# Moving operands of TensorE placed 64 bytes short of the weights' residue modulo 256

## Chip, cores and metric

One core of one Trainium2 chip. The metric is device time in microseconds (us) of one execution. All work is in fp32: matrix products are made of three products of a tighter 4-byte format (fp32r), as told below.

## What is computed

One layer of a macaron block on x of 512 tokens by 1024 channels, then a last RMS norm:

```python
x = x + 0.5 * swiglu(rms_norm(x, ffn1_norm), w_gate1, w_up1, w_down1)      # 1024 -> 2816 -> 1024
h = rms_norm(x, mix_norm)
z, xbc, dt_raw, u = split(h @ w_in)                                       # 1024 -> 3600
y_ssd = ssd_group(z, xbc, dt_raw, ...)     # conv of 4 taps, SiLU, chunked scan of 16 heads, gate, group norm
y_pool = pool_group(u, ...)                # trailing means of 2/4/8/16 frames, 256x256 maps
x = x + concat(y_ssd, y_pool) @ w_out                                     # 2048 -> 1024
x = x + 0.5 * swiglu(rms_norm(x, ffn2_norm), w_gate2, w_up2, w_down2)
out = rms_norm(x, final_norm)
```

## The kernel before

Everything is kept with channels on the 128 partitions and the 512 tokens along a row, so that one tile of 128 channels is 2048 bytes of each partition. `xT` holds the eight tiles of x.

**Units.** The weights come in 199 units. A unit is 8 blocks of 128 by 128 (5 or 6 for the down projections), fetched by SyncE's queue into one of RING = 4 slots of `raw` (`fetch`). ScalarE rounds it into `whi` (line 498, `convert`), VectorE subtracts into `wlo` (line 743), and TensorE multiplies. Activations are split likewise: `xghi`/`xglo` for the input of a stage, `acthi`/`actlo` for the hidden layer of the two feed-forward parts, `mixhi`/`mixlo` for the output of the SSD group, `sp0`..`sp2` for the pooled channels.

**Products.** `products` is the inner loop of nearly all of it. For each block k of a unit it makes three matmuls of 512 columns into one PSUM bank: weights `whi` with moving `hi` (line 1150), `whi` with `lo` (line 1151), `wlo` with `hi` (line 1152). Each has its own weight load of 128 columns, recorded as PEld, which the chip starts while the matmul ahead of it streams. A unit of 8 blocks is 24 such matmuls. The opening (`part`, lines 1216, 1219, 1222) makes the first 96 of them in another order, the dt unit 16 with narrow weights, the pool maps 48 (lines 1406 to 1408), and the very last tile 132 with 256 columns (lines 1471 to 1473), in two halves of the tokens with the tile's transposes between.

**Order.** Opening and gate/up of the first feed-forward (moving `xghi`, `xglo`, to some 253 us), its down projection (`acthi`, `actlo`, to 377), the mixer (`xghi`, `xglo` again, with small transposes of line 1274, decay rows, states of line 1284 and scans between the units; then `mixhi`, `mixlo` from 622 to 666), gate/up of the second feed-forward (`xghi`, to 907) and its down projection (`acthi`, to the end). The order of work on each engine is written out by hand and held by semaphores; it has no planner.

**Addresses.** The tensors of `sb(...)` are stacked one after another in each partition. The allocator puts the first, `raw`, at byte 1152. `raw`, `whi`, `wlo`, `xT`, `xghi`, `xglo` are 16,384 bytes each:

| tensor | start | start modulo 256 | role in TensorE |
|---|---|---|---|
| `whi`, `wlo` | 17536, 33920 | 128 | weights; a block is 512 bytes |
| `xghi`, `xglo` | 66688, 83072 | 128 | moving; a tile is 2048 bytes |
| `sumsq`, `ones`, `ident`, `causal` | 105600 to 108672 | 128 | weights or moving |
| `base` | 110016 | 192 | start of everything below |
| `acthi`, `actlo` | base, base + 44 KB | 192 | moving |
| `mixhi`, `mixlo`, `sp0`..`sp2`, `xsT`, `bT`, `ebuf`, `cbuf`, `acs_split`, `xst` | base + whole multiples of 256 | 192 | moving, or weights of transposes |

`base` is the end of the stack rounded up to a multiple of 64. All blocks and tiles are multiples of 256 bytes long, so every operand of these tensors has the residue of its tensor. The last tensor on `base` ends at 226,496; the allocator's limit is 229,368.

Of the kernel before, what the change touches and what calls it, by code (L numbers as in the profile page):

```python
# [23 lines left out]
P = 128  # L24
# [23 lines left out]

RING = 4
UB = 8  # L50
DOWN = (6, 6, 5, 5)
DOWN0 = (0, 6, 12, 17)

# [46 lines left out]
def block(tile):  # L100
    return slice(tile * P, (tile + 1) * P) if isinstance(tile, int) else bass.ds(tile * P, P)
# [6 lines left out]
def build(nc, t, out):  # L108
    with ExitStack() as ctx:
        def sb(name, shape, dt=F32):  # L110
            return ctx.enter_context(nc.sbuf_tensor(name, shape, dt))
# [4 lines left out]

        raw = sb("w_raw", [P, RING, UB, P])
        whi = sb("w_hi_part", [P, RING, UB, P], F32R)
        wlo = sb("w_lo_part", [P, RING, UB, P], F32R)
        xT = sb("xT", [P, DK * S])  # L120
        xghi = sb("xghi", [P, DK * S], F32R)
        xglo = sb("xglo", [P, DK * S], F32R)
        rstd = sb("rstd", [P, S])
# [13 lines left out]
        tok_rms = sb("tok_rms", [P, 2, NC])  # L137


        base = (nc.sbuf_base + 63) // 64 * 64  # L140

        def at(name, offset, shape, dt=F32):
            return nc.alloc_sbuf_tensor_at(name, shape, dt, offset=base + offset)
# [112 lines left out]
        def slot(m):  # L256
            return m % RING
# [27 lines left out]
        def _(sp):  # L285
            def fetch(m, i, src, blocks=UB, width=P):

                sp.wait_ge(w_hi, i * RING + (m - RING + 1))
                sp.wait_ge(w_lo, i * RING + (m - RING + 1))
                dst = raw[:, slot(m), 0:blocks, :]  # L290
                if width != P:
                    dst = raw[:, slot(m), :, :].rearrange("p (g c) n -> p g (c n)", c=width // P)
                sp.dma_start(dst, src).then_inc(landed[slot(m)], 16)

            def ffn_fetch(f, m0):
# [10 lines left out]
                with sp.Fori(0, DK) as i:  # L306
                    for j in range(4):
                        fetch(m0 + N_GU + j, i, wd[f][:, DOWN0[j]:DOWN0[j] + DOWN[j], block(i)], DOWN[j])

# [12 lines left out]
            def half_weight(m, h):  # L322
                ks = slice(h * (UB // 2), (h + 1) * (UB // 2))
                sp.dma_start(raw[:, m, ks, :], (wg, wu)[m % 2][0][:, ks, block(m // 2)]).then_inc(
                    (half_landed, landed)[h][m], 16)
# [163 lines left out]
        def _(act):  # L489
# [44 lines left out]
            def first_hi_half(m, h):  # L534

                act.wait_ge((half_landed, landed)[h][m], 16)
                ks = slice(h * (UB // 2), (h + 1) * (UB // 2))
                act.activation(whi[:, m, ks], raw[:, m, ks], ACT.Copy).then_inc((first_hi, w_hi)[h], 1)
# [597 lines left out]
        def _(pe):  # L1136
            def products(bank, m, i, blocks, hi, lo, k0, first=True, last=True, ready=None,
                         order=None, midway=None):

                pe.wait_ge(w_hi, i * RING + (m + 1))  # L1140
                pe.wait_ge(w_lo, i * RING + (m + 1))
                s = slot(m)
                for n, k in enumerate(order or range(blocks)):
                    if midway and n == blocks // 2:
                        midway()
                    if ready:
                        pe.wait_ge(ready[0], ready[1] + n + 1)
                    h, l = hi[:, cols(k0 + k)], lo[:, cols(k0 + k)]
                    w, wl = whi[:, s, k, :], wlo[:, s, k, :]
                    pe.matmul(bank, w, h, start=first and n == 0, stop=False)  # L1150
                    pe.matmul(bank, w, l, start=False, stop=False)  # L1151
                    mm = pe.matmul(bank, wl, h, start=False, stop=last and n == blocks - 1)  # L1152
                mm.then_inc(unit_done, 1)
# [17 lines left out]
            def down(f, m0, i, behind=None, tiles=2):  # L1171
                for e in range(tiles):
                    d = i * 2 + e
                    for j in range(4):
                        if j == 0:
# [3 lines left out]
                            else:  # L1179
                                pe.wait_ge(x_ready, d + (DK * (2 * f + 1) - 1))  # L1180
                        pe.wait_ge(act_lo, FT * f + DOWN0[j] + DOWN[j])
                        products(PB[4 + e][:, :], m0 + N_GU + 4 * e + j, i * 2, DOWN[j], acthi, actlo, DOWN0[j],
                                 first=j == 0, last=j == 3)
# [277 lines left out]
            for h in range(2):  # L1461
                for j in range(4):
                    m = M_FFN2 + N_GU + 4 * (DK - 1) + j
                    pe.wait_ge(w_hi, m + 1)
                    pe.wait_ge(w_lo, m + 1)
                    for k in range(DOWN[j]):
                        t0 = (DOWN0[j] + k) * S + h * HALF
                        hi, lo = acthi[:, t0:t0 + HALF], actlo[:, t0:t0 + HALF]
                        bank = PB[LAST_BANK[h]][:, 0:HALF]
                        first, last = j == 0 and k == 0, j == 3 and k == DOWN[3] - 1  # L1470
                        pe.matmul(bank, whi[:, slot(m), k, :], hi, start=first, stop=False)  # L1471
# [30 lines left out]
```

## Time and profile before

| | |
|---|---|
| median of 2 runs | 1041.89 us (1041.59 to 1042.2) |
| the profiled execution: its own time | 1042.32 us |
| its span from first to last instruction | 1040.6 us |
| granted TensorE clock, mean | 0.997 of 2.4 GHz |
| busy: PE, PEld, DVE, ACT, POOL | 1031.2, 847.3, 559.6, 380.4, 179.1 us |
| data moved by DMA | 99.09 MB, 95 GB/s over the span |

PE is TensorE's matmuls, PEld its weight loads, DVE VectorE, ACT ScalarE, POOL GpSimd. A matmul's booked duration overlaps the next one's, and its end is modelled; the distance between two starts says how fast a stream runs. PEclk is the clock that the chip granted to TensorE, as a share of 2.4 GHz.

### The profile page before, as it was taken

To read this page: it belongs to the slowest core of one execution; us is meant where nothing else is said; L and a number is where in the kernel's file an instruction comes from. 1 tells how busy PE (TensorE), PEld (TensorE's weight loads), DVE (VectorE), ACT (ScalarE), POOL (GpSimd) and SP (SyncE) were. 2 spreads that over 40 slices of the span, in tenths; PEclk is the share of its full clock that TensorE was granted. 3 is DMA by queue.
4 is the path that set the end of the run, shared out by engine and by line. 5 is a ranking of instruction groups with operands and counts; after the bars stand their busy time and mean duration, and the time that the engine had idled before them with its cause. 6 is when DMAs were issued, how large, how long until landed. Compare 5 with 4: busy or idle time off the path is not lost.

```text
span 1040.6 us, 13577 instructions
## 1 busy us (share of the span) xinstructions
PE 1031.2 (99%) x4798; PEld 847.3 (81%) x4798; DVE 559.6 (54%) x686; ACT 380.4 (37%) x489; POOL 179.1 (17%) x166
## 2 busy tenths in 40 slices
PE   9999999999999999999999999999999999999997
PEld 7888888888888878878787888888888888888887
DVE  5544444444344468786799795554444444433432
ACT  6433223322333337652234753432333223332332
POOL 1110110101001032221063451110101101101100
PEclk9999999999999999999999999999999999999998
DMA  6533323322333343222222233333333332233222
GB/s 184 150 113 101 101 86 95 101 83 68 99 98 96 101 124 100 82 81 70 73 81 81 62 101 101 101 101 90 92 101 101 96 87 89 79 109 95 86 68 81
DMA packets 188873, 99.09 MB, mean 95 GB/s; under 512 B 3780, under 2 KB 188200, under 8 KB 188840
## 3 DMA queue, kind: packets, MB, share of 16 engines
q1 hardware_dynamic: 188168, 97.60, 32.3%
q10 hardware_dynamic: 672, 1.05, 0.3%
q8 instruction: 21, 0.34, 0.1%
q14 instruction: 12, 0.10, 0.0%
HBM read 96.54 MB, written 2.10 MB: 95 GB/s over the span
## 4 chain that ended last, share of the span: by engine, by line
PE 96%; DVE 3%; issue 1%; ACT 1%; POOL 0%; ACTq 0%; POOLq 0%
PE bank L1150 29%; PE bank L1152 29%; PE bank L1151 29%; PE bank L1222 1%; PE bank L1216 1%; PE bank L1219 1%; PE bank L1471 1%; PE bank L1284 0%; PE bank L1306 0%; PE bank L1472 0%; PE bank L1473 0%; PE bank L1274 0%; DVE w_lo_part L743 0%; DVE ebuf L903 0%; PE bank L1190 0%
## 5 line engine op out<-in xcount | busy, mean ns | idle before, releaser
L1150 PE MATMUL bank<-xghi,w_hi_part 128*128 128x512 f32 x960 | 377.4, 393 | 0.0
L1152 PE MATMUL bank<-xghi,w_lo_part 128*128 128x512 f32 x960 | 373.8, 389 | 0.0
L1151 PE MATMUL bank<-xglo,w_hi_part 128*128 128x512 f32 x960 | 373.6, 389 | 0.0
L743 DVE TENSOR_TENSOR w_lo_part<-w_raw,w_hi_part 128x1024 fp32r<-128x1024 f32 x194 | 253.9, 1309 | 192.8 <-ACT w_hi_part L498 187.5
L498 ACT ACTIVATE w_hi_part<-w_raw 128x1024 fp32r<-128x1024 f32 x194 | 203.8, 1051 | 196.2 <-PE bank L1152 194.7
L1150 PEld LDWEIGHTS bank<-xghi,w_hi_part 128*128 128x128 f32 x960 | 180.2, 188 | 39.9 <-issue 2.8
L1151 PEld LDWEIGHTS bank<-xglo,w_hi_part 128*128 128x128 f32 x960 | 180.3, 188 | 38.4 <-issue 1.2
L1152 PEld LDWEIGHTS bank<-xghi,w_lo_part 128*128 128x128 f32 x960 | 180.2, 188 | 37.5
L1150 PE MATMUL bank<-acthi,w_hi_part 128*128 128x512 f32 x330 | 130.5, 396 | 0.0
L410 POOL TENSOR_TENSOR gate_buf<-gate_buf,rstd 128x512 f32<-128x512 f32 x44 | 57.1, 1298 | 424.5 <-ACT gate_buf L521 424.5
L1152 PE MATMUL bank<-acthi,w_lo_part 128*128 128x512 f32 x330 | 129.4, 392 | 0.0
L1151 PE MATMUL bank<-actlo,w_hi_part 128*128 128x512 f32 x330 | 128.1, 388 | 0.0
L524 ACT ACTIVATE acthi<-act 128x512 f32 (+1 forms) x44 | 27.8, 632 | 170.9 <-DVE act L766 170.9
L521 ACT ACTIVATE gate_buf<-gate_buf 128x512 f32<-128x512 f32 x44 | 27.8, 632 | 150.5 <-DVE gate_buf L763 150.5
L397 POOL TENSOR_TENSOR sumsq<-sumsq,sq 128x512 f32<-128x512 f32 x23 | 32.8, 1427 | 257.8 <-ACT sq L509 257.8
L1152 PEld LDWEIGHTS bank<-acthi,w_lo_part 128*128 128x128 f32 x330 | 61.9, 188 | 14.5
L1151 PEld LDWEIGHTS bank<-actlo,w_hi_part 128*128 128x128 f32 x330 | 62.0, 188 | 13.6
L1150 PEld LDWEIGHTS bank<-acthi,w_hi_part 128*128 128x128 f32 x330 | 62.0, 188 | 12.2
L766 DVE TENSOR_TENSOR act<-bank,gate_buf 128x512 f32<-128x512 f32 x44 | 30.4, 690 | 71.1 <-PE bank L1152 68.9
L763 DVE TENSOR_TENSOR gate_buf<-bank,rstd 128x512 f32<-128x512 f32 x44 | 30.4, 691 | 62.7 <-PE bank L1152 62.6
L768 DVE TENSOR_TENSOR actlo<-act,acthi 128x512 f32 (+1 forms) x44 | 30.5, 693 | 39.7 <-ACT acthi L524 39.7
L748 DVE SCALAR_TENSOR_TENSOR xglo<-xT,par,xghi (+1 forms) x24 | 25.6, 1078 | 25.6 <-ACT xghi L502 25.5
(223 smaller groups left out, 805.0 us busy)
## 6 DMA issues: line engine op xcount, KB each, us to landing
w_raw<-in_ffn_w_gate SPq DMA_DIRECT2D x42, 512.0 KB, 3.8
w_raw<-in_ffn_w_up SPq DMA_DIRECT2D x42, 512.0 KB, 3.8
w_raw<-in_w_in SPq DMA_DIRECT2D x29, 512.0 KB, 3.8
w_raw<-in_ffn_w_down SPq DMA_DIRECT2D x32, 384.0 KB, 3.2
w_raw<-in_ffn_w_down SPq DMA_DIRECT2D x32, 320.0 KB, 3.0
w_raw<-in_w_out SPq DMA_DIRECT2D x16, 512.0 KB, 3.6
out<-xtok SPq DMA_DIRECT2D x4, 512.0 KB, 3.4
xload<-in_x SPq DMA_DIRECT2D x3, 512.0 KB, 7.0
```

The lines of the kernel that those rows point to most:

```text
L397: pool.tensor_tensor(sumsq[:, :], sumsq[:, :], sq[:, e, :], ALU.add).then_inc(sum_own, 1)
L410: pool.tensor_tensor(gsilu[:, e, :], gsilu[:, e, :], rstd[:, :], ALU.mult).then_inc(g_r, 1)
L498: act.activation(whi[:, slot(m)], raw[:, slot(m)], ACT.Copy).then_inc(w_hi, 1)
L521: act.activation(gsilu[:, e, :], gscaled[:, e, :], ACT.Silu).then_inc(g_silu, 1)
L524: act.activation(acthi[:, cols(i * 2 + e)], act32[:, e, :], ACT.Copy).then_inc(act_hi, 1)
L743: dve.tensor_tensor(wlo[:, slot(m)], raw[:, slot(m)], whi[:, slot(m)].bitcast(F32), ALU.subtract).then_inc(w_lo, 1)
L763: dve.tensor_tensor(gscaled[:, e, :], PB[j][:, :], rstd[:, :], ALU.mult).then_inc(g_scaled, 1)
L766: dve.tensor_tensor(act32[:, e, :], PB[j][:, :], gsilu[:, e, :], ALU.mult).then_inc(act_ready, 1)
L768: dve.tensor_tensor(actlo[:, cols(i * 2 + e)], act32[:, e, :], acthi[:, cols(i * 2 + e)].bitcast(F32), ALU.subtract).then_inc(act_lo, 1)
L1150: pe.matmul(bank, w, h, start=first and n == 0, stop=False)
L1151: pe.matmul(bank, w, l, start=False, stop=False)
L1152: mm = pe.matmul(bank, wl, h, start=False, stop=last and n == blocks - 1)
```

## The change

Three edits, all to addresses. A tensor of padding, 48 elements or 192 bytes a partition, is put on the stack after `xT` so that `xghi` begins at residue 128 + 192 = 320, that is 64, modulo 256. `xglo` and all that is stacked behind it follow: `ones`, `ident`, `causal`, `sumsq` too come to 64. `base` is rounded up to the next address of residue 64 and not to the next multiple of 64; it goes from 110016 to 110400, so that all tensors on it move by 384 bytes. `raw`, `whi`, `wlo` and `xT` stay where they are. No instruction is added, removed or moved.

```diff
@@ -48,6 +48,8 @@
 
 RING = 4
 UB = 8
+LANES = 256
+WEIGHT_LANE = 128
 DOWN = (6, 6, 5, 5)
 DOWN0 = (0, 6, 12, 17)
 
@@ -118,6 +120,13 @@
         whi = sb("w_hi_part", [P, RING, UB, P], F32R)
         wlo = sb("w_lo_part", [P, RING, UB, P], F32R)
         xT = sb("xT", [P, DK * S])
+        def start_at(residue):
+
+            lane = (residue - nc.sbuf_base) % LANES
+            if lane:
+                sb(f"lane{nc.sbuf_base}", [P, lane // 4])
+
+        start_at(WEIGHT_LANE + 192)
         xghi = sb("xghi", [P, DK * S], F32R)
         xglo = sb("xglo", [P, DK * S], F32R)
         rstd = sb("rstd", [P, S])
@@ -137,7 +146,7 @@
         tok_rms = sb("tok_rms", [P, 2, NC])
 
 
-        base = (nc.sbuf_base + 63) // 64 * 64
+        base = nc.sbuf_base + (WEIGHT_LANE + 192 - nc.sbuf_base) % LANES
 
         def at(name, offset, shape, dt=F32):
             return nc.alloc_sbuf_tensor_at(name, shape, dt, offset=base + offset)
```

## Rows read from the trace of the kernel before

**Rows 1.** The page: busy us by engine, and the chain that ended last.

```profile
PE 1031.2 (99%) x4798; PEld 847.3 (81%) x4798; DVE 559.6 (54%) x686; ACT 380.4 (37%) x489; POOL 179.1 (17%) x166
...
PE 96%; DVE 3%; issue 1%; ACT 1%; POOL 0%; ACTq 0%; POOLq 0%
```

**Rows 2.** Waits of TensorE: us in total, times, longest.

```profile
PE bank L1190 <- POOL ones L368: 1.1, 1, 1.1
PE bank L1222 <- DVE w_lo_part L781: 0.6, 1, 0.6
...
PE bank L1216 <- ACT xghi L502: 0.3, 1, 0.3
```

**Rows 3.** Three stretches of TensorE: length, busy (count), PEclk, DMA share, GB/s.

```profile
98.00:250.00 152.00, 152.00 (x672) 1.00 0.31 91
256.00:370.00 114.00, 114.00 (x499) 1.00 0.35 102
740.00:900.00 160.00, 160.00 (x707) 1.00 0.31 91
```

**Rows 4.** Line 1150 in 98:135 and 255:372: durations min/median/max, first and last start.

```profile
L1150 PE MATMUL bank<-xghi,w_hi_part x55: 389/389/389, 98.2 to 134.9; 128*128 128x512 f32 x55
...
L1150 PE MATMUL bank<-acthi,w_hi_part x171: 394/394/394, 254.6 to 371.4; 128*128 128x512 f32 x171
```

**Rows 5.** Timeline of TensorE from 402 to 407: start us, booked us.

```profile
402.60 0.60 PE L1274 MATMUL bank<-ident,bT 128*128 128x128 f32 x4
...
403.27 0.39 PE L1151 MATMUL bank<-xglo,w_hi_part 128*128 128x512 f32 x1
...
404.65 0.39 PE L1151 MATMUL bank<-xglo,w_hi_part 128*128 128x512 f32 x1
404.88 0.39 PE L1152 MATMUL bank<-xghi,w_lo_part 128*128 128x512 f32 x1
...
406.92 0.39 PE L1152 MATMUL bank<-xghi,w_lo_part 128*128 128x512 f32 x1
```

**Rows 6.** The page's groups and its DMA issues (KB, us to landing).

```profile
L743 DVE TENSOR_TENSOR w_lo_part<-w_raw,w_hi_part 128x1024 fp32r<-128x1024 f32 x194 | 253.9, 1309 | 192.8 <-ACT w_hi_part L498 187.5
...
L763 DVE TENSOR_TENSOR gate_buf<-bank,rstd 128x512 f32<-128x512 f32 x44 | 30.4, 691 | 62.7 <-PE bank L1152 62.6
...
w_raw<-in_ffn_w_gate SPq DMA_DIRECT2D x42, 512.0 KB, 3.8
```

**Rows 7.** TensorE's groups by form: count, busy us, mean ns, idle before.

```profile
L1150 PE MATMUL bank<-xghi,w_hi_part 128*128 128x512 f32 x960 | 377.4, 393 | 0.0
...
L1150 PE MATMUL bank<-acthi,w_hi_part 128*128 128x512 f32 x330 | 130.5, 396 | 0.0
...
L1150 PE MATMUL bank<-mixhi,w_hi_part 128*128 128x512 f32 x64 | 25.2, 394 | 0.0
...
L1471 PE MATMUL bank<-acthi,w_hi_part 128*128 128x256 f32 x44 | 12.4, 282 | 0.0
...
L1216 PE MATMUL bank<-xghi,w_hi_part 128*128 128x512 f32 x32 | 10.4, 421 | 0.3 <-ACT xghi L502 0.3
...
L1284 PE MATMUL bank<-xst,btok 128*128 128x512 f32 x12 | 5.8, 592 | 0.0
```

**Rows 8.** Timeline of TensorE at 449.67: four matmuls of line 1284 merged.

```profile
449.67 1.88 PE L1284 MATMUL bank<-xst,btok 128*128 128x512 f32 x4
```

**Rows 9.** Timeline of TensorE in the last tile's two halves, then PEld's share.

```profile
1018.43 0.28 PE L1471 MATMUL bank<-acthi,w_hi_part 128*128 128x256 f32 x1
...
1021.83 0.28 PE L1471 MATMUL bank<-acthi,w_hi_part 128*128 128x256 f32 x1
...
1028.10 0.28 PE L1471 MATMUL bank<-acthi,w_hi_part 128*128 128x256 f32 x1
...
1030.93 0.28 PE L1471 MATMUL bank<-acthi,w_hi_part 128*128 128x256 f32 x1
...
1019.00:1025.00 6.00, 6.00 (x55) 6.00 (x54) 0.42 (x1) 0.67 (x2) 0.26 (x1) 1.00 0.00 0
```

## Prediction

> **What bounds the kernel now.** I read the page from the top. TensorE is busy for 1031.2 of 1040.6 us, VectorE for 54% and ScalarE for 37%; the chain of work that ended last is 96% TensorE [rows 1]. The waits of TensorE for other engines are next: there are six, 3.2 us in all, the longest 1.1 us at the very start and the shortest 0.3 [rows 2]. So time goes only if the matmuls follow each other faster. Busy time cannot say that, because a matmul of 512 columns is booked at 389 ns while the next starts after 227; I therefore count starts.
>
> At the clock granted in the long stretches (1.00 of 2.4 GHz, [rows 3]) 512 columns at one a cycle are 512/2.4 = 213.3 ns. With `xghi`/`xglo` as moving operand, line 1150 starts 55 times from 98.2 to 134.9 us, and three matmuls lie between two of its starts: 36.7/(54x3) = 226.5 ns. The finer timeline gives 404.88 to 406.92 us over 9 matmuls: 226.7. With `acthi`/`actlo`, line 1150 starts 171 times from 254.6 to 371.4: 116.8/(170x3) = 229.0 ns [rows 4, 5]. Counting whole stretches gives the same order: 160 us hold 707 matmuls (226 ns) with `xghi`, 114 us hold 499 (228 ns) with `acthi`, at the same clock [rows 3]. Only the address differs in a way I can name. The weight blocks begin at residue 128 modulo 256; `xghi` also does (relation 0), `acthi` at 192 (relation +64). So the relation can plausibly cost 2.3 ns of 227, though two stages differ in more than this.
>
> **The change part by part.** *Instructions and waits.* None is added or removed: two address shifts, +192 bytes from `xghi` on and +384 for everything on `base`. The last tensor then ends at 226,880, below the allocator's limit of 229,368. Cost 0. *Other engines' operands* move by multiples of 64 bytes. Were ScalarE, VectorE or GpSimd a few per cent slower by it, it would lie under TensorE: a unit of 24 products lasts 24 x 227 = 5.4 us, and VectorE works in it for one 1309 ns subtraction and, in the gate/up stages, on average one and a half passes of 690 ns: 2.3 us [rows 6]. Even at 213 ns a matmul the unit is 5.1 us. DMAs of a unit land in 3.8 us, four units ahead. I take 0, range 0 to 1 us (the waits of rows 2 a third longer).
>
> *Relation of moving operand to weights*, the real term. Counts [rows 6, 7]: relation 0 now: 3x960 (`xghi`), 3x32 in the opening, 16 of the dt unit: 2992 matmuls of 512 columns. Relation +64 now: 3x330 (`acthi`), 3x64 (`mixhi`), 48 pool products: 1230, and 132 of 256 columns. All come to -64, which no 512-column stream of this trace has. The 128-column transposes go the other way, from -64 (`ident` against `xsT`) to 0; some 110 of them at 109 ns start to start [rows 5] are 12 us, and 5% of that either way is 0.6 us: I take 0. Bounds from rows:
> - Lower: nothing lost at all. The one 512-column form that reads slower, plain f32 at line 1284, takes 1.88 us for four, of which the last is booked at 592: (1880-592)/3 = 429 ns, or 214.7 per 512 cycles [rows 7, 8]. Then 2992 x 12.0 + 1230 x 14.2 = 35.9 + 17.5 = 53 us less.
> - Upper: the slow state that the trace does show. The 256-column products of the last tile run at (1021.83-1018.43)/30 = 113.3 ns in the first half and (1030.93-1028.10)/24 = 117.9 ns in the second, with one residue and one code [rows 9]. 117.9 is 10.5% over its 106.7; 512 columns at that rate are 235.8. After an interruption 512-column products also run slower and then settle: six of them in 403.27 to 404.65 us, 230 ns each, before the 226.7 [rows 5]. Then 2992 x 9.1 + 1230 x 6.8 = 27.2 + 8.4 = 36 us more.
> - Between: 226.7 ns is 17/16 of 213.3, and 113.3 is 17/16 of 106.7. Two widths and two relations (0, +64) reach the same 17/16; that speaks for a rate of the 4-byte stream itself, one cycle per 16 columns, with collisions with weight reads on top (0 at relation 0 once settled, 2.3 ns at +64). It is no proof: with 256 columns PEld is booked for the whole of 1019 to 1025 [rows 9], so 113.3 may be the weight loads' own pace.
>
> I take the floor of 17/16 for all: 1230 x (229.0-226.7 = 2.3) = 2.8 us, and 84 of the 132 half-width ones from 117.9 to 113.3, 0.4 us: 3.2 us less. The settling after interruptions I leave as it is: 6 x 3.3 = 20 ns a place, so that sixty places would be 1.2 us. The profiled execution has 1042.3 us, 1.7 above its span and 0.4 above the median 1041.9: 1042.3 - 3.2 = 1039.1, on the median 1038.7. I say 1039.
>
> Here a rule speaks against the change having any effect. The two stages above differ by 2.3 ns a matmul. The Trainium skill (SBUF — State Buffer, "Who interferes with whom") says that TensorE has two independent read ports, one for the moving operand and one for weights, and never waits on anyone; by it the sum is 0 and the time stays 1042. The rows agree that busy neighbours do not matter, and leave open why 227 and 229 differ.
>
> **The rivals.**
> *B: the 17/16 is itself a collision, and -64 takes it away.* A weight block is 512 bytes; if its reads and the moving reads go through the same lanes, 13.4 ns may be what each load costs, and moving operands that trail by a lane may miss it. For: the trace's relation seems to matter already; plain f32, which takes twice the time per column, loses only 1.4 ns per 213. Against: 17/16 at both widths and both relations seen; settled stages show the loss in every matmul, whichever of the two weight tensors is loaded. All of it gone is 1042 - 53 = 989; half is 1015; I price it at 1000.
> Beside it: the Trainium skill (TensorE: Matmul & The Clock Gate, "Back-to-back issue gap") gives N/2.4 + 2.5 = 215.8 ns for an isolated bf16 gap; by it 2992 x 10.9 + 1230 x 13.2 = 49 us go, for 993. No settled 512-column row here reaches it.
> *C: -64 behaves as +64.* All relation-0 streams go from 226.7 to 229.0: 2992 x 2.3 = 6.9 us, nothing gained elsewhere: 1049. For: it is the nearest relation in size. Against: whether the moving read leads or trails the weight read need not be symmetrical.
> *D: slower.* With the moving read a lane behind, it runs into the weight read from the start of every load and never settles: the state that now lasts some six matmuls after an interruption, or all of the second half in rows 9, becomes permanent. Place: the inner products, lines 1150 to 1152. Price up to 36 us: 1078; it decides for "slower" from 232.3 ns a matmul (2992 x 5.6 + 1230 x 3.3 = 21 us). For: such a state is in the trace and lasted over 4 us in the last tile. Against: both relations seen leave it in 512-column streams.
> *E: the address has no effect* (the two stages differ by something else, such as the distance between high and low halves): 1042.
>
> **How the numbers follow.** A, the floor everywhere, 1039: 0.34. B, 989 to 1015: 0.26. C, 1049: 0.18. D, 1064 to 1078: 0.12. E, 1042: 0.10. The two per cent that a measurement can tell from no change is 21 us. B gives faster 0.26; A, C and E give same 0.62; D gives slower 0.12. The range: from 1039 down into B, leaving out only its full removal (about 0.1), and up past C to the foot of D (about 0.08 left out): 995 to 1060. The likeliest case alone spans 1036 to 1042 (with the transients gone, or 226.7 reached only in part).
>
> **What would show it.** Right: line 1150 to 1152 booked at 389 ns with `acthi` and `mixhi` too (now 394 settled); starts 226.7 apart in all stages; the first down projection (528 products, 121 us) 1.2 us shorter; gate/up stages unchanged. B: all of them booked below 389 and over 720 starts in a 160 us stretch of gate/up. C: 392 to 397 in the `xghi` groups, in a repeating triple like 232, 226, 229. D: 397 or more, and no settling after the transposes. The prediction is wrong if the `xghi` stages change by more than 1 ns a matmul, since the floor is what I carry over to a residue that no row shows; a change of VectorE's or ScalarE's mean durations with new waits of TensorE would refute the step that costs these at nothing.

## The result, and the profile after

| | before | changed |
|---|---|---|
| median | 1041.89 us | 1064.55 us |
| ratio, 95% interval | | 1.0216 (1.0199 to 1.0232) |
| span of the profiled execution | 1040.6 | 1063.1 |
| granted clock | 0.997 | 0.998 |

The kernel became 22.7 us slower. The prediction said 1039 and no more than 1060: it was wrong in size and in sign. The page of the changed kernel, busy time and the chain that ended last (lines of the kernel are now nine further down: 1150 to 1152 are 1159 to 1161):

```profile
PE 1054.1 (99%) x4798; PEld 847.5 (80%) x4798; DVE 559.5 (53%) x686; ACT 380.5 (36%) x489; POOL 179.0 (17%) x166
...
PE 98%; DVE 1%; ACT 0%; issue 0%; POOL 0%; ACTq 0%; POOLq 0%
```

Against [rows 1] one number moved: PE, from 1031.2 to 1054.1, 22.9 us, as much as the whole kernel lost. VectorE, ScalarE, GpSimd and the weight loads are as busy as before to 0.2 us, and the instructions are as many. TensorE's waits (us in total, times, longest):

```profile
PE bank L1199 <- POOL ones L377: 1.1, 1, 1.1
PE bank L1231 <- DVE w_lo_part L790: 0.6, 1, 0.6
...
PE bank L1225 <- ACT xghi L511: 0.3, 1, 0.3
```

All stand in [rows 2] too, with the same lengths; there are five now, 2.8 us in all, where there were six, 3.2 us. So nobody keeps TensorE waiting longer than before; its own stream runs slower. The three stretches of [rows 3], and line 1159 in 98 to 135 us (durations min/median/max, first and last start):

```profile
98.00:250.00 152.00, 152.00 (x654) 1.00 0.31 91
256.00:370.00 114.00, 114.00 (x490) 1.00 0.32 96
740.00:900.00 160.00, 160.00 (x688) 1.00 0.31 92
```

```profile
L1159 PE MATMUL bank<-xghi,w_hi_part x54: 393/396/398, 97.6 to 134.7; 128*128 128x512 f32 x54
```

At the same granted clock 160 us now hold 688 matmuls and held 707; the `acthi` stretch holds 490 and held 499. Line 1159 starts every (134.7-97.6)/(53x3) = 233.3 ns, where [rows 4] gave 226.5, and its booked durations spread over 393 to 398 where they all were 389. The timeline around the same transposes as in [rows 5]:

```profile
411.33 0.39 PE L1161 MATMUL bank<-xghi,w_lo_part 128*128 128x512 f32 x1
...
412.27 0.60 PE L1283 MATMUL bank<-ident,bT 128*128 128x128 f32 x4
412.62 0.48 PE L1159 MATMUL bank<-xghi,w_hi_part 128*128 128x512 f32 x1
412.94 0.40 PE L1160 MATMUL bank<-xglo,w_hi_part 128*128 128x512 f32 x1
...
415.74 0.40 PE L1160 MATMUL bank<-xglo,w_hi_part 128*128 128x512 f32 x1
```

From 412.94 to 415.74 are 12 matmuls, 233.3 ns each, from the first on; before, six at 230 led over to 226.7. The four transposes are booked for 0.60 us together as before, although their relation went from -64 to 0. Summed over the whole trace from each start to the next of any matmul, the three lines with `xghi`/`xglo` took 658.1 us before and 675.7 now (+17.6), with `acthi`/`actlo` 227.2 and 231.5 (+4.3), with `mixhi`/`mixlo` 44.0 and 44.8 (+0.8), and the half-width products 16.1 and 15.9 (-0.3 unrounded). Together that is 22.4 of the 22.5 us by which the spans differ.

### The profile page after: what moved, and what is told of

Read it like the earlier page. It is cut to its first block, busy times and chain, and to the rows that moved or that the text cites. A ratio compares the mean times of both kernels' runs of the same rounds, so it can differ in the third digit from the quotient of the medians.

```text
span 1063.1 us, 13577 instructions
## 1 busy us (share of the span) xinstructions
PE 1054.1 (99%) x4798; PEld 847.5 (80%) x4798; DVE 559.5 (53%) x686; ACT 380.5 (36%) x489; POOL 179.0 (17%) x166
## 4 chain that ended last, share of the span: by engine, by line
PE 98%; DVE 1%; ACT 0%; issue 0%; POOL 0%; ACTq 0%; POOLq 0%
PE bank L1159 30%; PE bank L1160 30%; PE bank L1161 30%; PE bank L1315 1%; PE bank L1231 1%; PE bank L1225 1%; PE bank L1228 1%; PE bank L1320 0%; PE bank L1293 0%; PE bank L1480 0%; PE bank L1481 0%; PE bank L1482 0%; PE bank L1283 0%; PE bank L1199 0%; PE bank L1415 0%; PE bank L1215 0%
## 5 line engine op out<-in xcount | busy, mean ns | idle before, releaser
L1159 PE MATMUL bank<-xghi,w_hi_part 128*128 128x512 f32 x960 | 383.0, 399 | 0.0
L1160 PE MATMUL bank<-xglo,w_hi_part 128*128 128x512 f32 x960 | 379.6, 395 | 0.0
L1161 PE MATMUL bank<-xghi,w_lo_part 128*128 128x512 f32 x960 | 379.6, 395 | 0.0
L1160 PE MATMUL bank<-actlo,w_hi_part 128*128 128x512 f32 x330 | 130.4, 395 | 0.0
```

## Experiments

The theory now: what counts is the distance, modulo 256, from the residue of the weights to that of the moving operand (the relation). Rivals: the absolute residue 64 is bad; or the two stages of the kernel before differed for another reason.

**Both kinds at relation 0** (all_0). Edits are shown against the changed kernel, here and below.

```diff
-        start_at(WEIGHT_LANE + 192)
+        start_at(WEIGHT_LANE + 0)
...
-        base = nc.sbuf_base + (WEIGHT_LANE + 192 - nc.sbuf_base) % LANES
+        base = nc.sbuf_base + (WEIGHT_LANE + 0 - nc.sbuf_base) % LANES
```

> All moving operands at relation 0 to the weights (residue 128, base too). Relation theory (the distance of moving operand and weights modulo 256 sets the rate; relation 0 runs at 226.7 ns a matmul, +64 at 229, -64 at 233.3): acthi and mixhi streams fall from 229.0 to 226.7, xghi stays; 1230 x 2.3 = 3 us less than before: 1039. Rival, what made acthi slower than xghi in the kernel before is something else (distance of high and low halves, stage): 1042, acthi still at 229.

Measured: 1040.43 us against 1042.33 for the kernel before, ratio 0.9983 (0.9973 to 0.9992). Line 1159 in the down projection, and the last tile (start, booked):

```profile
L1159 PE MATMUL bank<-acthi,w_hi_part x172: 389/389/389, 255.2 to 371.5; 128*128 128x512 f32 x172
```

```profile
1018.11 0.28 PE L1480 MATMUL bank<-acthi,w_hi_part 128*128 128x256 f32 x1
...
1021.71 0.28 PE L1480 MATMUL bank<-acthi,w_hi_part 128*128 128x256 f32 x1
```

The `acthi` stream went to (371.5-255.2)/(171x3) = 226.7 ns. Of the 3 us, 2 arrived: the 512-column products took 2.4 us less, but the half-width ones, at (1021.71-1018.11)/30 = 120.0 ns, are slower than either state of [rows 9] and took 0.6 us more. Of the relations tried in the whole kernel, 0 is the best place for 512 columns and a bad one for 256.

**The same relation -64 at other absolute residues** (weights_up): 64 bytes of padding ahead of `raw`, so that the weights begin at 192 and the moving operands at 128.

```diff
+        sb("lane_w", [P, 16])
         raw = sb("w_raw", [P, RING, UB, P])
...
-WEIGHT_LANE = 128
+WEIGHT_LANE = 192
```

> Weights move to residue 192 and all moving operands to residue 128, so the relation is again -64 but no absolute residue is that of the change. Relation theory: as the changed kernel, 1064 to 1065, 233 ns a matmul. Rival, the absolute residue of the moving operand decides (128 is good, 64 bad): 226.7 ns and 1039 to 1042.

Measured: 1064.69 us, ratio 1.0216 (1.0199 to 1.0233), the same as the changed kernel. The inner products of the gate/up stage (`whi` with `xghi`, now line 1160) have the spread and the starts of the changed kernel's:

```profile
L1160 PE MATMUL bank<-xghi,w_hi_part x54: 393/396/398, 97.6 to 134.7; 128*128 128x512 f32 x54
```

The residue 128 of the moving operand, good before, is as bad as 64 once the weights are at 192. So the residue of the moving operand alone does not decide. Case E of the prediction, that addresses do nothing, was refuted by the change itself.

**Relations +128 and +64 for all** (all_p128, all_p64), by the numbers in the two lines of the first diff.

> All moving operands at relation +128 (residue 0). No row shows it. Relation theory with collisions that depend on who leads: between the values of +64 and -64, 229 to 233 ns, 1048 to 1065. Rival, the distance alone counts and 128 is farthest: either free of collisions, at or under 226.7 ns and 1039 or less, or the worst, over 1065. Absolute residue theory gives no number.

> All at relation +64, the price of the prediction's case C. Sweep: xghi streams 2992 x 2.3 = 7 us more, less up to 1 us for settling: 1048 to 1049, with a triple like 232, 226, 229 in the gate/up stages. Rival, the value 229 belongs to the down projections alone: 1042, 227 in the gate/up stages.

Measured: 1062.65 us, ratio 1.0203 (1.0186 to 1.022), at +128, inside the 1048 to 1065 of the relation theory and outside both of the rival's; 1048.11 us against 1042.00, ratio 1.006 (1.0043 to 1.0077), at +64, as the theory said. The same stretch, 740 to 900 us, of these two (+128, then +64):

```profile
740.00:900.00 160.00, 160.00 (x688) 1.00 0.32 93
```

```profile
740.00:900.00 160.00, 160.00 (x701) 1.00 0.31 91
```

The gate/up stages at +64 show the triple that [rows 4]'s down projection averages, near 226, 229 and 232 ns. At +128 the streams have no single value: over 24 matmuls without an interruption they take between 232.1 and 233.3 ns, where the kernel with all at 0 has 226.7 and the changed one 233.3 nearly everywhere.

**One part at a time** (xg_only, base_only).

In xg_only `xghi` and `xglo` stay at -64 and `base` goes back to +64; in base_only it is `xghi` that goes back, to 0.

```diff
-        base = nc.sbuf_base + (WEIGHT_LANE + 192 - nc.sbuf_base) % LANES
+        base = nc.sbuf_base + (WEIGHT_LANE + 64 - nc.sbuf_base) % LANES
```

```diff
-        start_at(WEIGHT_LANE + 192)
+        start_at(WEIGHT_LANE + 0)
```

> Only xghi, xglo and what is stacked behind them move to relation -64; base keeps +64. If the relation costs what the sweep shows (226.7 at 0, 233.3 at -64), the xghi streams lose 2992 x 6.6 = 20 us, less about 1 us because the settling phases of the kernel before are already as slow: 1060 to 1062, and acthi stays at 229. Rival, the loss of the changed kernel sits in the down projections and the mixer's other products: 1042 to 1047.

> Only base moves, from relation +64 to -64; xghi and xglo keep 0. Sweep: 1230 x (233.3 - 229.0 = 4.3) = 5 us more, less 0.3 us for the half-width products of the last tile: 1046 to 1047. The two one-part kernels should add up to the changed kernel's 22 us. Rival, the parts interact (transposes between weights on base and ident): they add up to less or more by over 3 us.

Measured: 1059.26 and 1047.28 us against 1042.00, ratios 1.0165 (1.0148 to 1.0182) and 1.0053 (1.0036 to 1.007). 17.3 + 5.3 = 22.6 us, the changed kernel's 22.7. The parts add up. `xghi` costs 17.3 and not the 20 of my sum, mainly because the matmuls after interruptions were already slow before: in the traces of before and changed, the first 12 distances of two starts after each interruption of the `xghi`/`xglo` stream average 238.1 and 242.3 ns, 4.2 more, and all later ones 226.8 and 233.3, 6.6 more. In each, only the stream that was moved changed: the stretches 740:900 and 256:370 of xg_only, then of base_only:

```profile
256.00:370.00 114.00, 114.00 (x500) 1.00 0.33 96
740.00:900.00 160.00, 160.00 (x687) 1.00 0.32 92
```

```profile
256.00:370.00 114.00, 114.00 (x490) 1.00 0.35 102
740.00:900.00 160.00, 160.00 (x707) 1.00 0.32 93
```

**TensorE alone, 16 relations** (micro1). The layer is left out: ScalarE fills weights and 16 moving tiles, then only TensorE works. The weights stay at residue 128 and one moving tile serves all three matmuls of a triple.

```python
for i in range(n):
    w = (whi, whi, wlo)[i % 3]
    pe.matmul(PB[0][:, :], w[:, i // 3 % UB, :], mv[d], start=i == 0, stop=i == n - 1)
```

> Not the layer: TensorE alone runs series of 48 matmuls of 512 columns in the 4-byte format, weights at residue 128, the moving operand in 16 places from relation 0 to +240 in steps of 16 bytes; first upwards without pause, then downwards with four small fp32 matmuls ahead of each series. No other engine works meanwhile. Relation theory: 226.7 ns at 0, 229 at 64, 233 at 192, and the steps between show at what grain (16, 32 or 64 bytes) it changes. If the loss needs the other engines' accesses, all series run alike. If the floor of 17/16 is a collision too, some relation falls under 226.7 towards 213.3; if it is the stream's own rate, none does.

Mean distance of two starts in the second half of each series, second pass (512 columns, 128 weight columns):

| relation | 0 | 16 | 32 | 48 | 64 | 80 | 96 | 112 |
|---|---|---|---|---|---|---|---|---|
| ns | 226.7 | 231.7 | 233.3 | 233.3 | 228.9 | 231.1 | 233.3 | 231.1 |
| relation | 128 | 144 | 160 | 176 | 192 | 208 | 224 | 240 |
| ns | 233.3 | 233.3 | 234.2 | 233.3 | 233.3 | 230.0 | 233.3 | 236.7 |

Timeline of relations 240, 192, 64 and 0, ten triples between the two rows of each:

```profile
207.84 0.40 PE L68 MATMUL bank<-mv,wlo 128*128 128x512 f32 x1
...
214.94 0.40 PE L68 MATMUL bank<-mv,wlo 128*128 128x512 f32 x1
```

```profile
244.10 0.40 PE L68 MATMUL bank<-mv,wlo 128*128 128x512 f32 x1
...
251.10 0.40 PE L68 MATMUL bank<-mv,wlo 128*128 128x512 f32 x1
```

```profile
342.72 0.39 PE L68 MATMUL bank<-mv,wlo 128*128 128x512 f32 x1
...
349.58 0.39 PE L68 MATMUL bank<-mv,wlo 128*128 128x512 f32 x1
```

```profile
390.81 0.39 PE L68 MATMUL bank<-mv,wlo 128*128 128x512 f32 x1
...
397.61 0.39 PE L68 MATMUL bank<-mv,wlo 128*128 128x512 f32 x1
```

7.10, 7.00, 6.86 and 6.80 us over 30 matmuls. The kernel's values come back with no other engine at work and at most 2 GB/s of DMA while the series run: 226.7, 228.9, 233.3. So the loss is TensorE's own. None of the 16 is below 226.7. The values do not lie on a smooth curve, but most are simple fractions of one step: 233.3-226.7 is 6.7 ns, the time of 16 columns at 2.4 GHz, and 16 columns are 64 bytes of the moving operand. Over the 213.3 of the bare columns, relation 0 loses 2 steps a matmul, +64 loses 7 in three matmuls (2.3 each), 192 three.

The first pass, upwards and without pause, has the same 16 addresses and agrees within 0.1 ns on 13 of them. The other three settle elsewhere: 128 at 232.3 ns and not 233.3, 208 at 234.7 and not 230.0, and 240 at 226.7 and not 236.7. Relation 240 in the first pass, again 30 matmuls between the first start of the two rows:

```profile
194.46 0.61 PE L68 MATMUL bank<-mv,whi 128*128 128x512 f32 x2
...
201.26 0.61 PE L68 MATMUL bank<-mv,whi 128*128 128x512 f32 x2
```

6.80 us, as short as at relation 0 and 0.30 less than at the same addresses in the second pass. So at some relations there is more than one settled rate, and what ran ahead of a series can decide which one it takes: the relation alone does not. At the relations on which this case rests every 512-column series with 128 weight columns agrees, in micro1 to micro3: 0 has 226.7 ns in all nine, 64 has 228.9 in all three, 192 has 233.3 in all nine.

**Other widths** (micro2): the same with weights of 128, 64 and 32 columns and 512, 384 and 256 moving columns.

> Not the layer: TensorE alone, series of 48 matmuls, with weights of 128, 64 and 32 columns, moving operands of 512, 384 and 256 columns, at relations 0, 64, 128, 192 and 208 (that order, four small fp32 matmuls ahead of each series). Stream theory (17/16 is the 4-byte stream's own rate, and only what lies above it is collision): at relation 0 every weight width gives 226.7, 170 and 113.3 ns for the three column counts; at 192 the excess of 6.7 ns shrinks with the weights' width to 3.3 and 1.7. Collision theory (each weight line read costs the stream time at every relation): at relation 0 with 512 columns 226.7, 220 and 216.7 ns for 128, 64 and 32 weight columns.

With 128 weight columns at relation 0: 226.7, 173.3 and 120.0 ns. Timeline of 384 and of 256 columns, four triples between the rows:

```profile
84.34 0.33 PE L72 MATMUL bank<-mv0x,wlo 128*128 128x384 f32 x1
...
86.42 0.33 PE L72 MATMUL bank<-mv0x,wlo 128*128 128x384 f32 x1
```

```profile
130.13 0.28 PE L72 MATMUL bank<-mv0x,wlo 128*128 128x256 f32 x1
...
131.57 0.28 PE L72 MATMUL bank<-mv0x,wlo 128*128 128x256 f32 x1
```

2.08/12 and 1.44/12. The bare columns are 213.3, 160.0 and 106.7 ns, so the loss at relation 0 is 13.3 ns at all three widths. My 17/16 would have given 170.0 and 113.3: the stream theory is refuted. The collision theory as I had put it falls too. At 512 columns and relation 0 the narrow weights give 230.0 (64 columns) and 231.7 (32), slower than the full 226.7 and not 220 and 216.7. Here 208 took 234.7 ns with 128 weight and 512 moving columns, as in the first pass of micro1.

**What else could matter** (micro3).

> Not the layer: TensorE alone, series of 48 matmuls with four small fp32 ones ahead. In order: relations 0 and 192; then 4, 8, 12, 244, 248, 252; then 256, 512, 1024 and 448; then for 0 and for 192 each: four PSUM banks in turn, every matmul a group of its own, always the same weight block, weight blocks downwards, weight blocks upwards one a matmul; then 496, 480, 448, 416, 352, 320 moving columns at 0 and 192; then 24 matmuls in plain fp32 at 0 and 192. So far a settled series loses a whole number of 6.67 ns steps (16 columns, 64 bytes of the moving read) over its repeating pattern: 2 steps a matmul at relation 0, 3 at 192. If the loss comes from the reads of SBUF modulo 256, then 256, 512 and 1024 run as 0 (226.7) and 448 as 192 (233.3), PSUM banks and groups change nothing, and plain fp32, with twice the time for a column, loses under 2 ns at both relations. If PSUM has a part in it, the series with banks in turn or separate groups run faster, near 214 to 220. If the weight blocks' step has a part in it, always the same block differs from upwards. A loss that is constant per matmul gives N/2.4 + 13.3 at 0 for the other widths; a rate gives N/2.4 x 17/16.

- Relations 256, 512 and 1024: 226.7; 448: 233.3. The period is 256 bytes as far as tried.
- Four PSUM banks in turn, or every matmul a group of its own, or always the same weight block, or blocks downwards or upwards: 226.7 at relation 0 and 233.3 at 192, each. At these two relations PSUM and the order of the blocks have no part in it.
- Relations 4, 8 and 12: 236.7, 233.3 and 228.9; 244, 248 and 252: 233.3, 230.0 and 226.7. In these series, one for each, four bytes past the best place cost 10 ns.
- 496, 480, 448, 416, 352 and 320 columns at relation 0: 16.7, 16.7, 16.1, 15.0, 14.4 and 13.3 ns over the bare columns. At 192: 20.0, 16.0, 15.5, 13.3, 13.3 and 13.3. It is a cost a matmul, of 13.3 to 20 ns, and not a share of the width; for most of these widths 192 is no worse than 0.
- Plain fp32: each matmul is recorded twice, at 429 ns a record at both relations, 2.5 over the 426.7 of two cycles a column. Of the two relations tried neither is better.

**Is it the size of the weight load?** (micro4)

> Not the layer: TensorE alone, series of 36 matmuls with four small fp32 ones ahead, at all 16 relations from 0 to 240 in steps of 16 bytes; first with weights of 64, then 32, then 16 columns (moving 512), then with 128 weight columns and 256 moving. Question: are the two steps (13.3 ns) that 512 columns lose even at relation 0 the collision of the stream with a weight load's read? If so, a load of 16 columns, an eighth of the read, leaves most relations free: 213.3 to 216 ns for some of the 16, and a mean well under that of 128 columns (232.7). If the number of weight columns read does not matter (only that a load is there, or where its first reads fall), the 16-column series spread over 226.7 to 235 as well, with none under 226.7.

The mean over the 16 relations is 230.6, 231.7 and 231.5 ns with 64, 32 and 16 weight columns. With 128 it was 231.9 in the first pass of micro1 and 232.3 in the second, not the 232.7 of the expectation. None of the 48 series is under 226.7. With 16 columns the good relation is 32 (226.7) and relation 0 has 231.6; with 64 columns 48, 160 and 208 are good. With 128 weight and 256 moving columns two relations, 112 and 192, reach 113.3 and the other 14 lie between 116.9 and 120.0; but 192 took 117.8 in micro2, again two rates at one relation. So an eighth of the weight columns saves under 1 ns of 19 in the mean, less than the 10 ns between the two rates of relation 240. The good places of this run lie elsewhere for each number of weight columns. Since single series can settle in more than one way, it does not show how much of that is the width's doing.

## Why the prediction was wrong, step by step

- *TensorE's rate alone decides; other engines' addresses cost nothing.* Right: busy times of the others are unchanged, waits too, and TensorE alone shows the same values.
- *The relation matters, not the stage.* Right for the kernels, and shown by weights_up, all_p64 and the sweep; at relations such as 240 it is not the whole of it. The trace of before gave a true hint with 227 against 229. A rule said otherwise: the Trainium skill (SBUF — State Buffer, "Who interferes with whom") has TensorE's two read ports independent and never waiting. The runs here disagree: the same moving residue, 128, gives 226.7 ns with the weights at 128 and 233.3 with the weights at 192. They do not show which access stands in the way.
- *"I take the floor of 17/16 for all."* This is the step that failed, twice. I read 226.7 and 113.3 as one rate of the stream because both are 17/16 of the bare columns. That was a coincidence, and the two came from different relations, 0 and +64: 226.7 is 13.3 ns a matmul, two steps, and 113.3 is 6.7, one step. At relation 0 384 columns take 173.3 and not 170, and 256 take 120.0. Being no rate, the floor could not be carried to a residue that no row showed. At -64 the 512-column streams lose three steps: 233.3. The sum had 3.2 us less, and the kernel took 22.7 us more. The prediction's own sign of being wrong, more than 1 ns a matmul in the `xghi` stages, came: 6.6 ns.
- *"84 of the 132 half-width ones from 117.9 to 113.3, 0.4 us."* This small part came true, with a wrong count: in the trace of before 66 of them ran at 117.9 and the other 66 at 113.3, at the same residues; in the changed kernel all 132 settle at 113.3, for 0.3 us less. That they would was no more than the same floor, so it was luck.
- *The upper bound.* It held: 235.8 ns was assumed as the slowest stream and 233.3 came. That is in part luck, since relation 4 took 236.7 in micro3. Of the bound's 36 us, 2992 x 6.6 + 1230 x 4.3 = 25 us are what the sweep gives, less what the matmuls after interruptions had lost already, 22.7. A slow stretch was in the trace, after each interruption, and I had priced it.
- *Rival D* had the right sign, place and threshold (slower from 232.3 ns); its price of 1064 to 1078 holds the measured 1064.6 at its foot. Its picture, a moving read that runs into the weight read of each load, is not shown: with an eighth of the weight columns the mean loss is nearly the same. It had 0.12, and my range ended at 1060 just short of it. With two known relations of a period with at least four places, the two seen were no sample of the third; the range should have reached at least to the foot of D and past it.
- *Case C*, -64 behaves as +64: refuted, 233.3 ns and not 228.9.
- *Rival B*, the loss taken away: refuted. None of the series of 512 columns, whatever the relation, weight width, PSUM bank or block order, came under 226.7. The Trainium skill (TensorE: Matmul & The Clock Gate, "Back-to-back issue gap") gives N/2.4 + 2.5 for an isolated matmul, 215.8 for 512 columns of bf16. No run here has bf16, and the 4-byte format never comes nearer than 11 ns to it.
- *Case C's price*, 1049 for +64 everywhere: measured 1048.1. *Case A's*, relation 0 for acthi, 1039: the 512-column part came (226.7), the half-width part went the other way (120 and not 113.3), 1040.4 in all, against 1042.3 for the kernel before in that comparison.
- *The transposes*, costed at nothing: they run at the same distances before and after.

What stays open: where the two steps at the best place come from, which access it is that the moving read meets, if it meets one, and why one relation can settle at two rates. Other PSUM banks, other blocks and idle neighbours leave them in place, and no weight width tried goes below them. A matmul without any weight load ahead was not tried.

## What to carry to other kernels

A kernel of 4-byte matmuls that already keeps TensorE 99% busy can still be made faster or slower by the start addresses of its operands: this one took 1040.4 us with all at relation 0 and 1064.6 at -64. Count starts, since the booked busy share says 99% either way. For 512 columns with 128 weight columns put moving operand and weights at the same residue modulo 256. For other widths sweep it in a kernel of TensorE alone, which at 0, +64 and -64 gave what the whole kernel did. Run each series more than once, behind different ones, and trust only a relation that settles at one rate each time. And do not carry a floor to a case that no row shows because two of its values share a ratio: a third width would have told a rate from a cost a matmul.

## What the runs showed of the hardware that I had not expected

- Averaged over its repeating pattern, the distance of two starts in a settled stream of 512 and 128 weight columns lies 2, 2.3, 2.5, 2.7, 3 or 3.5 steps of 6.7 ns (16 columns) above the bare columns for most relations, with patterns like 231/236 or 226/229/232. Single distances are no whole steps.
- The same addresses can settle at two rates, and stay there for tens of matmuls: relation 240 at 226.7 and 236.7 ns, 208 at 234.7 and 230.0, and with 256 columns +64 at 113.3 and 117.9 in the last tile of the kernel before.
- Four bytes decide: relation 252 has 226.7 ns, 0 has 226.7, and 4 has 236.7.
- The good relations depend on the moving width: with 128 weight columns 0 always has 226.7 at 512 columns, and is among the slowest at 256 (120.0), where 112 and 192 had 113.3 in one run.
- Plain fp32, with two records of 429 ns for 512 columns, was the same at relations 0 and 192.
